# Weight chunks land in the slots of their low parts: five ring slots in place of four slots and two landing buffers, and chunk loops in bodies of twenty or written out

## The reference

```python
x = first_block(x, ...)    # rmsnorm, w_in, differential + chunked attention, gates,
                           # w_branch, w_out, then peer(): retrieval of experts
x = second_block(x, ...)   # swiglu FFN, hybrid mixer (RG-LRU + window attention), swiglu FFN

def peer(xn, wq, keys, u, v):     # per token: 8 heads x 16 experts out of 16384
    ...                           # product keys, two top_k, softmax g
    hid = jnp.einsum('thkd,td->thk', u[e], xb)
    a = jax.nn.gelu(hid, approximate=False) * g
    return jnp.einsum('thk,thkd->td', a, v[e])

def swiglu(x, w_gu, w_down):
    gate, up = jnp.split(x @ w_gu, 2, axis=-1)
    return (jax.nn.silu(gate) * up) @ w_down
```

## Time and profile before

| | |
|---|---|
| median of 3 runs | 1537.48 us (1533.52 to 1541.29) |
| the profiled execution, its own time | 1530.73 us |
| its span, first to last instruction | 1529.2 us |
| granted TensorE clock, mean over the span | 0.994 |
| busy: PE, DVE, ACT | 1495.4, 1114.7, 738.3 us |
| weights moved (SP's queue) | 259.01 MB |

### The profile page before, as it was taken

The page is one execution under the profiler, slowest core; times in us unless marked ns, Lnnn a source line. Parts: engine busy times, 40 slices in busy tenths (PEclk is TensorE's granted clock), DMA queues, the critical chain, the costliest instruction groups (busy, mean ns, idle before and its releaser), DMA issues. The chain is left out here.

```text
span 1529.2 us, 27764 instructions
## 1 busy us (share of the span) xinstructions
PE 1495.4 (98%) x10806; PEld 1378.3 (90%) x10806; DVE 1114.7 (73%) x1579; ACT 738.3 (48%) x850; POOL 267.9 (18%) x306
## 2 busy tenths in 40 slices
PE   8999999999999999999999999999899999999998
PEld 7888998999999999998888888889899888899986
DVE  5657666699999989837676777677677576777753
ACT  4366753545454455444444444445344457644431
POOL 1100000000000111025565456540000010000000
PEclk9999999999999999999999999999999999999999
DMA  6553343666665777797877778774556543255551
GB/s 250 211 193 139 118 150 105 214 245 237 235 235 207 255 234 272 259 325 286 288 287 280 298 289 299 285 257 152 190 197 212 195 143 127 97 190 196 193 200 74
DMA packets 56535, 329.47 MB, mean 215 GB/s; under 512 B 7520, under 2 KB 7568, under 8 KB 25088
## 3 DMA queue, kind: packets, MB, share of 16 engines
q1 hardware_dynamic: 36144, 259.01, 47.0%
q0 software_dynamic: 20304, 69.21, 13.1%
HBM read 294.64 MB, written 33.55 MB: 215 GB/s over the span
## 5 line engine op out<-in xcount | busy, mean ns | idle before, releaser
L954 DVE TENSOR_TENSOR wl<-raw,wh 128x2048 fp32r<-128x2048 f32 x244 | 586.9, 2406 | 257.0 <-ACT wh L552 255.8
L552 ACT CAST wh<-raw 128x2048 fp32r<-128x2048 f32 x244 | 466.2, 1911 | 400.6 <-DMA raw<-in_wstream 333.0
L1878 PE MATMUL ub<-xh,wh 128*128 128x256 f32 x2168 | 613.1, 283 | 12.7 <-DVE fg L1069 7.2
L1879 PE MATMUL ub<-xl,wh 128*128 128x256 f32 x2168 | 604.8, 279 | 0.0
L1880 PE MATMUL ub<-xh,wl 128*128 128x256 f32 x2168 | 604.8, 279 | 0.0
L1878 PEld LDWEIGHTS ub<-xh,wh 128*128 128x128 f32 x2168 | 411.5, 190 | 21.9 <-DVE fg L1069 7.8
L1879 PEld LDWEIGHTS ub<-xl,wh 128*128 128x128 f32 x2168 | 412.8, 190 | 0.1
L1880 PEld LDWEIGHTS ub<-xh,wl 128*128 128x128 f32 x2168 | 411.3, 190 | 0.0
L1878 PE MATMUL acc<-wh,ah 128*128 128x512 f32 x512 | 200.0, 391 | 0.2
L1880 PE MATMUL acc<-wh,al 128*128 128x512 f32 x512 | 199.2, 389 | 0.0
L1879 PE MATMUL acc<-wl,ah 128*128 128x512 f32 x512 | 199.2, 389 | 0.0
(11 more groups left out here) (373 smaller groups left out, 1667.4 us busy)
## 6 DMA issues: line engine op xcount, KB each, us to landing
raw<-in_wstream SPq DMA_DIRECT2D x244, 1024.0 KB, 4.9
gates<-gst POOLq DMA_DIRECT2D x16, 1024.0 KB, 15.5
gl_in<-gates POOLq DMA_DIRECT2D x64, 256.0 KB, 4.9
hidden<-hid POOLq DMA_DIRECT2D x60, 256.0 KB, 4.5
hid<-hidden POOLq DMA_DIRECT2D x60, 256.0 KB, 4.8
resid<-in_x SPq DMA_DIRECT2D x2, 512.0 KB, 3.9
raw<-in_wstream SPq DMA_DIRECT2D x2, 512.0 KB, 7.2
rb<-in_rel POOLq DMA_DIRECT2D x1, 1024.0 KB, 8.7
```

The costliest lines, as they stand in the source:

```text
L552: act.copy(wh[:, slot, :], raw[:, slot % RAW, :]).then_inc(w_high, 1)
L954: v.tensor_tensor(wl[:, slot, :], raw[:, slot % RAW, :], wh[:, slot, :].bitcast(F32), ALU.subtract).then_inc(w_low, 1)
L1878: pe.matmul(dst, sh, mh, start=first, stop=False)
L1879: pe.matmul(dst, sh, ml, start=False, stop=False)
```

## The change

The buffer `raw` gets no space of its own any more: it is laid over `wl`, so that a chunk lands in the slot in which its low part will stand, and DVE subtracts in place. The space of the two landing slots gives a fifth slot to `wh` and `wl` (10 slots of 8 KB in a partition before and after). A load of chunk c therefore waits for PE to have finished chunk c-5, and no longer for the low part of chunk c-2; ACT's split no longer waits for `c_done`. The first five chunks are loaded at the start with no wait. AHEAD stays 3. Since five slots do not come round in bodies of four, the loops over `pv` have bodies of twenty chunks, and the loops over the last chunks of `pu` and over `gu` are written out.

```diff
-RAW = 2
-RING = 4
-AHEAD = RING - 1
+RING = 5
+AHEAD = 3
...
+VBODY = 4 * RING
...
-        raw = sb("raw", [P, RAW, CW])
         wh = sb("wh", [P, RING, CW], F32R)
+
+        st = ExitStack()
+        raw = sb("raw", [P, RING, CW], at=st)
+        st.close()
         wl = sb("wl", [P, RING, CW], F32R)
...
-            sp.dma_start(raw[:, 1, :], stream[1]).then_inc(raw_in[1], 16)
-
-            def load(c, slot):
-                sp.wait_ge(w_low, c - RAW + 1)
-                sp.dma_start(raw[:, slot, :],
-                             stream[bass.ds(c, 1)].rearrange("a p n -> p (a n)")).then_inc(raw_in[slot], 16)
-
-            pairs = (NCH - RAW) // 2
-            with sp.Fori(0, pairs) as i:
-                for j in range(2):
-                    load(i * 2 + (RAW + j), j)
-            for c in range(RAW + 2 * pairs, NCH):
-                load(c, c % RAW)
+            for c in range(1, RING):
+                sp.dma_start(raw[:, c, :], stream[c]).then_inc(raw_in[c], 16)
+
+            with sp.Fori(0, NCH // RING - 1) as i:
+                for j in range(RING):
+
+                    sp.wait_ge(c_done, i * RING + (j + 1))
+                    sp.dma_start(raw[:, j, :], stream[bass.ds(i * RING + (RING + j), 1)]
+                                 .rearrange("a p n -> p (a n)")).then_inc(raw_in[j], 16)
...
-            def split(c, slot):
-
-                act.wait_ge(raw_in[slot % RAW], arrived(c, slot))
-                if not isinstance(c, int) or c >= RING:
-                    act.wait_ge(c_done, c - RING + 1)
-                act.copy(wh[:, slot, :], raw[:, slot % RAW, :]).then_inc(w_high, 1)
+            def split(c):
+
+                slot = c % RING
+                act.wait_ge(raw_in[slot], c // RING * 16 + 16)
+                act.copy(wh[:, slot, :], raw[:, slot, :]).then_inc(w_high, 1)
...
-                with act.Fori(1, 5) as i:
-                    for j in range(2, 6):
-                        ahead_at(i * 4 + (C + j), C + j)
-                        silu(i * 4 + (U + j), i * 4 + (nf + j), j % 2)
+                for j in range(6, FT):
+                    ahead(C + j)
+                    silu(U + j, nf + j, j % 2)
...
-                v.tensor_tensor(wl[:, slot, :], raw[:, slot % RAW, :], wh[:, slot, :].bitcast(F32),
+                v.tensor_tensor(wl[:, slot, :], raw[:, slot, :], wh[:, slot, :].bitcast(F32),
                                 ALU.subtract).then_inc(w_low, 1)
...
-                with v.Fori(1, 5) as i:
-                    for j in range(2, 6):
-                        ahead_at(i * 4 + (C + j), C + j)
-                        take(i * 4 + (C + j), (U + j) % 2, j % 2)
-                        finish(i * 4 + (U + j), i * 4 + (nf + j), j % 2, bass.ds(i * 4 + j, 1))
+                for j in range(6, FT):
+                    ahead(C + j)
+                    take(C + j, (U + j) % 2, j % 2)
+                    finish_first(j)
...
             pe.wait_ge(g_sb, GROUPS)
-            for j in range(4):
+            for j in range(VBODY):
                 value_step(0, j, first=j == 0)
-            with pe.Fori(1, 15) as i:
-                for j in range(4):
+            with pe.Fori(1, 60 // VBODY) as i:
+                for j in range(VBODY):
                     value_step(i, j)
             for j in range(3):
-                value_step(15, j)
+                value_step(60 // VBODY, j)
```

More of the change, by code:

```diff
@@ L265, in in_bank @@
             return k + 1 if k < 2 else (k | 1) + 1
-        raw_in = [sem(f"raw_in{k}") for k in range(RAW)]
+        raw_in = [sem(f"raw_in{k}") for k in range(RING)]
         first_in = sem("first_in")
@@ L741, in hidden_step @@
             def hidden_step(n, nmod):
-                ahead_at(n + CU, CU + nmod)
+                ahead(n + CU)
                 act.wait_ge(c_done, n + (CU + 1))
@@ L777, in _ @@
                     spread(g, g % 2)
-            with act.Fori((TOPK_U + SPREAD_U) // 4, 15) as i:
-                for j in range(4):
-                    hidden_step(i * 4 + j, j)
+            for n in range(TOPK_U + SPREAD_U, 60):
+                hidden_step(n, n)
             def high_step(n, nmod):
@@ L791, in _ @@
                 hidden_step(n, n)
[L793 to L799, removed]
-                for j in range(4):
-                    value_step(i, j)
-            for j in range(4):
-                value_step(15, j)
+            with act.Fori(0, 60 // VBODY) as i:
+                for j in range(VBODY):
+                    high_step(i * VBODY + (j + 1), j + 1)
+                    ahead_in(i, CV + j)
+            for n in range(60, 64):
+                if n < 63:
+                    high_step(n + 1, n + 1)
+                    ahead(n + CV)
             def ffn(gu, dn, nf, w, stage):
@@ L1447, in _ @@
                 gates_step(1, j)
-            with v.Fori((TOPK_U + SPREAD_U) // 4, 15) as i:
-                for j in range(4):
-                    ahead_at(i * 4 + (CU + j), CU + j)
+            for n in range(TOPK_U + SPREAD_U, 60):
+                ahead(n + CU)
             def lowpart(n, k):
@@ L1459, in _ @@
                     lowpart(0, 0)
-                ahead_at(n + CU, CU + n)
-            def value_step(i, j):
-                n = i * 4 + j
-                if not (isinstance(n, int) and n == 63):
-                    lowpart(n + 1, j + 1)
-                    ahead_at(n + CV, CV + j)
-            with v.Fori(0, 15) as i:
-                for j in range(4):
-                    value_step(i, j)
-            for j in range(4):
-                value_step(15, j)
+                ahead(n + CU)
+            with v.Fori(0, 60 // VBODY) as i:
+                for j in range(VBODY):
+                    lowpart(i * VBODY + (j + 1), j + 1)
+                    ahead_in(i, CV + j)
+            for n in range(60, 64):
+                if n < 63:
+                    lowpart(n + 1, n + 1)
+                    ahead(n + CV)
             def weigh(tt):
@@ L2092, in hidden_step @@
                     pe.wait_ge(hd_g, n - 1)
[L2093 removed]
+                unit_chunk(n + CU, CU + n, None, nmod)
             def turn_indices(tt):
@@ L2128, in _ @@
                     gates_step(at, j)
-            with pe.Fori((TOPK_U + SPREAD_U) // 4, 16) as i:
-                for j in range(4):
-                    hidden_step(i * 4 + j, j)
+            for n in range(TOPK_U + SPREAD_U, 64):
+                hidden_step(n, n)
             def value_step(i, j, first=False, last=False):
-                n = i * 4 + j
+                n = i * VBODY + j
                 pe.wait_ge(a_l, n + 1)
@@ L2164, in ffn @@
                 unit_chunk(C + 5, C + 5, U + 5, U + 5)
-                with pe.Fori(1, 5) as i:
-                    for j in range(2, 6):
-                        unit_chunk(i * 4 + (C + j), C + j, i * 4 + (U + j), U + j)
+                for j in range(6, FT):
+                    unit_chunk(C + j, C + j, U + j, U + j)
                 for k in range(9):
```

30 lines of the change are left out of this document (14 added, 16 removed).

## The result

| | before | changed |
|---|---|---|
| median | 1535.5 us (4 runs, 1531.08 to 1541.29) | 1513.09 us (4 runs, 1507.28 to 1516.46) |
| profiled execution, own time | 1530.73 us | 1513.73 us |
| a second set of runs | 1533.88 us (17 runs, 1527.60 to 1540.29) | 1512.25 us (4 runs, 1512.12 to 1512.36) |

The ratio is 0.9855 (95% interval 0.982 to 0.989), and in the second set 0.9860 (0.9831 to 0.9889). The change gives about 22 us. The direction and the FFN mechanism were right, and the size was not.

A forecast was written before the change was run, and what follows sets the result against it. PE was taken as the bound, with only its pace and few idle stretches counting. 14.5 us from the FFNs plus 0.5 elsewhere made 15.0, so 1537.5 became 1522.5 us, range 1514 to 1532.

The forecast's parts named there:

- The load's wait, in the FFNs: In gu1 and gu2, loads waiting for PE's chunk five back go out earlier and remove PE's waits: 14.5 us gained.
- The replay: Hand-carried order of the FFNs: some 0.2 of 3.38 us stays before gu1[8], and all three waits in gu2 go.
- The gain in other places where ACT waits for a landing is small: 0.5 us in all: Attention's start and the expert stretch: 0.5 us gained, between 0 and 2.
- That one ran 6.8 us below the median of the runs, so against the median: 1537.5 - 15.0: Whole kernel: the gain of 15.0 us on the profiled execution, taken off the runs' median, gives 1522.5 us.
- The lower end of the range: Whole kernel: 1514 us, with small terms at their upper bounds (2 and 2.7) and a median as low as the profiled run.
- The fifth slot: Slots of the weight chunks: given no term of its own, as the order is fixed by `ahead`, three chunks ahead.
- a load there has over 5 us until its split: Attention stretches: loads go out 3 to 6 us later than before, but are covered; without cover, 3 us once a stretch.
- The start: Three more full chunks queue behind the half chunk PE waits for: taken as 0, at most 1.5 us.
- Loops and code: FFN loops and written-out chunks: register instructions saved give nothing, and loading a quarter more code is hidden.
- The code rival: In `pv`, PE waits 3 us at its one jump back for three code packets: 12 us faster, 1525.5; chance 0.08.
- The subtraction in place: DVE's low part: costs nothing, bounds from -0.1 to 0 us on DVE, hidden in both.
- The pace rival: Matmuls of `pu` and the FFNs all at PE's slow pace: 24 us, giving 1546, slower than before; chance 0.05.

The follow-up runs named there:

- w_low_ffn: Changed kernel, loads written out on SP, each load from gu1 on also waiting for the low part of chunk c-2; 1520.24 us, 0.9922 of before.
- w_low_head: Changed kernel, loads written out on SP, each load up to gu1 also waiting for the low part of chunk c-2; 1521.72 us, 0.9911 of before.
- w_low_experts: Changed kernel with the old load rule (low part of chunk c-2) added for the chunks of pu and pv alone; 1517.06 us, 0.9896 of before.
- ring4: Changed kernel with four slots in place of five, loads written out on SP; 1650.25 us, 1.0771 of before.
- before_again: The kernel before, run and profiled once more with nothing changed; 1534.04 us, ratio 1.0001.
- after_again: The changed kernel, run and profiled once more with nothing changed; 1512.25 us, 0.9860 of before.
- before_flat: The kernel before with the loops of pu and gu written out and pv in bodies of twenty; 1536.44 us, 0.9999 of before.
- turn4: Changed kernel with four transposes in place of three in turn_indices, twice; 1507.22 us (one run).

## Why the prediction was right, and where it was wrong

- **How far off.** I said 1522.5 and it was 1513.1, 9.4 us less. Of that 7.4 is the gain (22.4 in place of 15.0) and 2.0 the starting point: a fourth run brought the median before from 1537.5 to 1535.5.
- **The load's wait, in the FFNs: right.** The load of gu1[8] went out at 1064.14 us, 0.2 us after gu1[3] was done; it landed at 1069.01, and its split ran at 1070.55 with no wait for it, 6.4 us behind the issue (I had said about 10). The replay left 0.2 us of the wait before gu1[8]; from its start to the next that chunk took 5.46 us in place of 5.44, so 0.02 was left. The clock stayed at 1.00. I gave the FFNs 14.5 us. With the pace of the matmuls taken out, the two traces differ there by 6.5 in gu1 (6.2 forecast) and by 7.7 in gu2 (8.3 forecast), together 14.2. The second pair of traces gives 6.3 and 7.9, the same sum. w_low_ffn, where the rule came back, returned 8.0 us in its median and 10.5 in its profile. Some 2 us of the 14.2 are there only because the clock fell in gu2 in both profiles of the kernel before, which it does not always do behind such a wait (see w_low_ffn above).
- **"The gain in other places where ACT waits for a landing is small: 0.5 us in all": this step failed.** It measured 9.5 us (w_low_head; some 6 between the profiles with the pace of the matmuls taken out, as below), and w_low_experts puts about half of it in the experts' chunks. I had reasoned that ACT's 333.0 us of waits cost nothing unless PE waits behind them, which is right, and then looked only for PE waiting for low parts, in one trace. What stands behind a waiting split on ACT is not only its low part but `ah`, `hid`, `pT` and the top-k's work, and PE wants those long before the chunk. The rows show this for `ah` in `pv`, and for `pT` in ring4; for the other places before the FFNs it is argued from the queues' order. The trace of before had the sign of it: the casts of `ah` that PE held back were 36 of 64, where an ACT that is really ahead has 62.
- **"That one ran 6.8 us below the median of the runs, so against the median: 1537.5 - 15.0": this step failed too.** It takes the distance between a good run and the median as fixed. It is not. The changed kernel's profiled run, 1513.73, lies 0.6 us above its median, so the two profiles differ by 17.0 us and the medians by 22.4. A late landing here and there costs the old kernel a chain; before_again's profile (1533.50, 21.3 us over after_again's) has, in sum, 2.7 us more of losses than the one I read, the pace of the matmuls taken out. That pace is worth another 3.5 us between the two profiles of the result, against the changed kernel.
- **The lower end of the range was added up wrong.** By the terms named for it, 1530.7 - 14.5 - 2 - 2.7, it is 1511.5 and not 1514. The measured time would lie above that, but by luck, since the term that was too small measured 9.5 and not 2.
- **The fifth slot, "no term of its own": misread.** Its value sat inside my load term, since I computed with c-5 throughout. ring4 shows that in-place landing without it would have cost 138 us against the changed kernel. The remark that in attention "a load there has over 5 us until its split" was true with five slots, and not with four.
- **The start: wrong sign.** I took 0, at most 1.5 us worse. The wait for the first low part is 1.3 us shorter, and by before_flat that comes with the form of the code; 0.4 of it is lost before, where `x` lands later, and the changed kernel is 0.8 us ahead after the first chunk.
- **Loops and code: right.** before_flat is 0.9999. q8 moved 82 packets in place of 65, and PE never paused in `pv`. The code rival of 3 us fell; by the half of the rule in the Trainium skill (Runtime: NRT & Kernel Launch, section Instruction fetch mechanics) that gives PE's buffer 2048 instructions nothing was to be expected, and the trace agrees: no idle time of PE stands at its one jump back over some 1000.
- **The subtraction in place: right** (the low part's mean is 2.321 in place of 2.406 us, and it is hidden).
- **The pace rival: real, but not of this change.** The paces of the two kernels' traces differ by 3.5 us in disfavour of the changed one (some 2400 of its 6960 matmuls of 256 columns at the slower pace, some 1600 before, at 0.0044 us each). It decided no sign.

With the pace taken out so, the profiles of the old kernel are 1523.8 and 1526.5 us, those of the changed one 1503.2 and 1503.0: a gain of 20.6 to 23.5. Of it the FFNs have 14.2, the start 0.8, and the rest, 6 to 8 us, is what late landings cost outside the FFNs: in `pv` through ACT's queue, as the rows show, and elsewhere by a way that is argued and not shown.

## What to carry to other kernels

An engine that prefetches must be asked what stands behind the prefetch in its queue, and not only whether the prefetched data are in time. Count how often its other work was early (waited for the bottleneck): here 36 or 22 of 64 went with a loss of 2 to 3 us in `pv`, and 62 of 64 with none. Let a load depend on the engine that frees the slot, PE here, and on nothing that itself waits for loads. And read two profiles of the kernel before, since one good run hides the losses that come by chance.

## What was not expected of the hardware

In these traces PE has two paces for one and the same stream at full clock, and in most stretches it keeps the one that it starts with. The rows are stretches of 70 us, columns as above, first of the changed kernel and then of turn4:

```profile
300.00:370.00 70.00, 70.00 (x597) 70.00 (x596) 67.53 (x153) 31.94 (x28) 6.49 (x12) 1.00 0.69 238
390.00:460.00 70.00, 70.00 (x620) 70.00 (x619) 69.40 (x156) 33.85 (x30) 6.77 (x13) 1.00 0.70 244
```

```profile
300.00:370.00 70.00, 70.00 (x620) 70.00 (x619) 69.41 (x148) 34.09 (x29) 7.02 (x13) 1.00 0.72 241
390.00:460.00 70.00, 70.00 (x620) 70.00 (x619) 69.38 (x141) 33.55 (x28) 7.02 (x13) 1.00 0.72 245
```

The first and third row are the same work at the same granted clock: 597 in 70 us are 0.1173 us each, 620 are 0.1129. In the earlier trace rows the kernel before has the slower pace from 390 us on, and it has the quicker one around 300; the changed kernel has it the other way round. That is no mark of the kernel, since before_again has it as the changed kernel does. In all thirteen profiles with three transposes between the two stretches exactly one of the two had the slower pace. In the long stretches of gu1 and gu2 the pace differs from profile to profile of one kernel (gu1 quick in one trace of the changed kernel and slow in the other, gu2 the reverse), and it changes only where PE has paused or done small products. Each of the long stretches, 600 to 860 matmuls, is worth 3 to 4 us, so a few of them could make up much of the 9 us between runs of one kernel; only the profiled runs can be looked at for it. What selects the pace is open.
